# The output gate of the gated linear attention: from the delta-rule stage's woven tiles back into the input projection

## What is computed

```python
for l in range(DEPTH):
    x = layer_norm(ALPHA * x + swiglu_half(x, ffn1...), ln1...)
    h = x @ w_in[l]
    (a_u, a_v, b_qkv, b_z, b_beta, b_decay,
     c_q, c_k, c_v, c_r, c_g) = jnp.split(h, split_at, axis=-1)
    out_a = spatial_gating(gelu(a_u), gelu(a_v), ...)
    out_b = gated_deltanet(b_qkv, b_z, ...)   # ends in: rms_norm(o) * silu(z)
    out_c = gla(c_q, c_k, c_v, c_r, c_g, ...) # ends in: rms_norm(o) * silu(r)
    x = layer_norm(ALPHA * x + concat(out_a, out_b, out_c) @ w_out[l], ln2...)
    x = layer_norm(ALPHA * x + swiglu_half(x, ffn2...), ln3...)
```

## The kernel before

| Stage | Slot | Products before |
|---|---|---|
| form | after the first spreads | 2 |
| form | p = 0, 1, 2, 3 | 3, 3, 3, 5 |
| units | after the mean's sums, after the square's sums | 5, 7 |
| units | after the key transposes (L2206) | 1 |
| units | after the gating's products (L2225) | 2 |
| units | after the scores (L2233) | 4 |
| units | after the outputs (L2240, L2245) | 4 |
| solve | after the first 32x32 products | 1 |
| solve | r = 0, 1, 2, 3 | 2 each |

## Time and profile before

### The profile page before, as it was taken

The page is one execution under the profiler, slowest core; times in us unless marked ns, Lnnn a source line. Parts: engine busy times, 40 slices in busy tenths (PEclk is TensorE's granted clock), DMA queues, the critical chain, the costliest instruction groups (busy, mean ns, idle before and its releaser), DMA issues.

```text
span 3838.6 us, 45043 instructions
## 1 busy us (share of the span) xinstructions
PE 3726.0 (97%) x18720; PEld 3064.0 (80%) x18720; DVE 2073.4 (54%) x3686; ACT 1354.8 (35%) x2088; POOL 86.1 (2%) x164
## 2 busy tenths in 40 slices
PE   8997999999999999999999999999999999999998
PEld 5985669999997678888887767788788877677886
DVE  5936767644457553334336775533553367765335
ACT  4424443222237442322223833322232228333222
POOL 0100001111100000000000000000000000000000
PEclk9998999999999999999999998999999999999999
DMA  6410003433311022233232211222222222112222
GB/s 223 151 61 1 23 23 124 124 129 127 117 64 48 23 88 96 96 108 101 96 99 83 88 45 44 83 99 99 88 96 94 98 88 83 51 50 88 97 96 83
DMA packets 92887, 333.38 MB, mean 87 GB/s; under 512 B 11364, under 2 KB 11532, under 8 KB 92428
## 3 DMA queue, kind: packets, MB, share of 16 engines
q1 hardware_dynamic: 77040, 278.10, 21.7%
q0 software_dynamic: 12800, 41.95, 3.6%
q10 hardware_dynamic: 2844, 10.44, 0.8%
HBM read 328.35 MB, written 2.10 MB: 86 GB/s over the span
## 4 chain that ended last, share of the span: by engine, by line
PE 90%; DVE 6%; ACT 2%; issue 1%; DMA 0%; PEldq 0%; ACTq 0%; DVEq 0%; PEld 0%; SPq 0%
PE PS L552 74%; PE PS L1108 2%; PE PS L554 2%; PE PS L1126 1%; PE PS L1654 1%; PE PS L2134 1%; PE PS L1466 1%; PE PS L1093 1%; PE PS L1009 1%; DVE silu_ctx L2587 1%; DVE arena L2585 1%; DVE H_r L734 0%; DVE XH L906 0%; PE PS L1096 0%; PE PS L1094 0%
## 5 line engine op out<-in xcount | busy, mean ns | idle before, releaser
L552 PE MATMUL PS<-arena_r,ring_hi 128*128 128x512 f32 (+1 forms) x6028 | 2024.1, 375 | 22.8 <-DVE H_r L734 20.2
L552 PE MATMUL PS<-arena_r,ring_r 128*128 128x512 f32 (+1 forms) x4556 | 1701.4, 373 | 0.0
L552 PEld LDWEIGHTS PS<-arena_r,ring_hi 128*128 128x128 f32 x6028 | 1125.9, 188 | 199.3 <-issue 27.3
L552 PE MATMUL PS<-H_r,ring_hi 128*128 128x512 f32 (+1 forms) x3084 | 1151.2, 373 | 0.0
L552 PEld LDWEIGHTS PS<-arena_r,ring_r 128*128 128x128 f32 x4556 | 855.6, 188 | 125.5
L398 DVE TENSOR_TENSOR ring_r<-ring,ring_hi 128x1024 fp32r<-128x1024 f32 x502 | 612.6, 1222 | 603.8 <-ACT ring_hi L389 603.5
L389 ACT ACTIVATE ring_hi<-ring 128x1024 fp32r<-128x1024 f32 x502 | 528.9, 1055 | 864.2 <-DMA ring<-weights_dram 856.2
L552 PEld LDWEIGHTS PS<-H_r,ring_hi 128*128 128x128 f32 x3084 | 580.3, 188 | 89.0 <-issue 2.6
L1823 ACT ACTIVATE arena<-PS 128x512 f32<-128x512 f32 x88 | 52.6, 598 | 519.2 <-PE PS L552 519.2
L1272 DVE SCALAR_TENSOR_TENSOR XH<-PS,mods,XH 128x256 f32<-128x256 f32 (+1 forms) x168 | 79.4, 518 | 232.6 <-PE PS L552 218.3
L353 DVE CAST arena_r<-arena 128x512 fp32r<-128x512 f32 (+1 forms) x184 | 74.2, 403 | 196.8 <-ACT arena L1319 193.7
(11 more groups left out here) (382 smaller groups left out, 3296.6 us busy)
## 6 DMA issues: line engine op xcount, KB each, us to landing
ring<-weights_dram SPq DMA_DIRECT2D x526, 512.0 KB, 3.3
rstd<-ada_later_dram POOLq DMA_DIRECT2D x54, 256.0 KB, 3.0
mean<-ada_later_dram POOLq DMA_DIRECT2D x53, 256.0 KB, 3.0
ada_extra<-ada_later_dram POOLq DMA_DIRECT2D x53, 256.0 KB, 3.0
XH<-xT_dram ACTq DMA_DIRECT2D x1, 3072.0 KB, 20.0
ring<-weights_dram ACTq DMA_DIRECT2D x4, 512.0 KB, 4.0
out_dram<-XH SPq DMA_DIRECT2D x8, 256.0 KB, 2.0
con<-second_dram ACTq DMA_DIRECT2D x1, 1536.0 KB
```

The lines of the kernel that those rows point to most:

```text
L552: ins = pe.matmul(PS[:, o.bank, 0:hi - lo], w[:, 0, :], x, **flags)
```

## The change

The two tiles of `c_r` leave the woven tiles and become two ordinary tiles of `in_plan` (split products, evacuated by ACT with SiLU straight from PSUM), placed ahead of the four GELU tiles. The order of the weights in `stream()` follows, and so do the side jobs of the projection: those that hung on tiles 14 to 18 now hang on tiles 16 to 20, behind the same neighbours as before. Four woven tiles are left, 32 products per layer, on banks 4, 4, 6, 7. The slots are now 2 and 3, 3, 2, 2 in form; 5, 7, 0, 1, 1, 1 in units; 1 and 1, 1, 1, 1 in solve. Two of ACT's six woven copies go (the first operation of `units_act` and the one ahead of the r loop in `solve_act`); the copy of woven tile 1 is therefore made after L2273. `rec_act` has four SiLUs left, none of them at n = 2.

```diff
-WOVEN_COLS = [(2048, 2560), (3088, 3344)]
-WOVEN_BANKS = (4, 4, 6, 7, 6, 7)
+WOVEN_COLS = [(2048, 2560)]
+WOVEN_BANKS = (4, 4, 6, 7)
...
-                s += ftiles(w, (0, 512)) + ttiles(w, (2832, 3088))
+                s += ftiles(w, (3088, 3344)) + ftiles(w, (0, 512)) + ttiles(w, (2832, 3088))
...
-            t[15]["beside_pe"] = gates_pe
+            t[17]["beside_pe"] = gates_pe
...
             t += [ftile(x_x, LAT, "dve", copy_dve(to_lat(d))) for d in (qg, kg)]
+            t += [ftile(x_x, LAT, "act", func_act(to_lat(rg[:, m, :]), ACT.Silu)) for m in range(2)]
             t += [ftile(x_x, LAT, "act", func_act(to_lat(d), ACT.Gelu_apprx_tanh)) for d in (up_[:, 0, :], up_[:, 1, :], vp_[:, 0, :], vp_[:, 1, :])]
...
-        woven_dst = [zp[:, m, :] for m in range(4)] + [rg[:, m, :] for m in range(2)]
+        woven_dst = [zp[:, m, :] for m in range(4)]
...
             ins.then_inc(ga_kt.sem, 1)
-            woven_pe(pe, 1)
             woven_copied_pe(pe, l, 2)
...
             ins.then_inc(sg_z.sem, 1)
-            woven_pe(pe, 2)
+            woven_pe(pe, 1)
...
                 ins.then_inc(ga_s.sem, 1)
-            woven_pe(pe, 4)
+            woven_pe(pe, 1)
...
             ins.then_inc(ga_o.sem, 1)
-            woven_pe(pe, 4)
+            woven_pe(pe, 1)
 
         def units_act(act, l):
 
-            woven_act(act)
             act.wait_ge(sg_mean.sem, sg_mean.next("act"))
...
-                woven_pe(pe, 5 if p == 3 else 3)
+                woven_pe(pe, 3 if p < 2 else 2)
...
                 ins.then_inc(so_z.sem, 1)
-                woven_pe(pe, 2)
+                woven_pe(pe, 1)
...
-            woven_act(act)
             for r in range(4):
                 act.wait_ge(so_z.sem, so_z.next("act"))
```

More of the change, by code:

```diff
@@ L1943, in in_plan @@
             t[13]["beside_act"] = lambda act: l2_roots_act(act)
[L1944 to L1950, removed]
+            t[16]["beside_dve"] = lambda dve: (l2_scale_dve(dve, 1), zero_rows_dve(dve, l))
+            t[16]["beside_pe"] = lambda pe: turn_rows_pe(pe, l)
+            t[17]["beside_act"] = lambda act: (turned_rows_act(act), high_rows_act(act))
+            t[17]["beside_pe"] = lambda pe: turn_keys_pe(pe, l)
+            t[18]["beside_dve"] = lambda dve: (key_rows_dve(dve, l), low_rows_dve(dve))
+            t[19]["beside_pe"] = lambda pe: turn_values_pe(pe, l)
+            t[20]["beside_dve"] = value_rows_dve
             return together(t, 4)
```

## The result

The changed kernel takes 3870.41 us (median of 4 runs, 3869.47 to 3870.91), the kernel before 3841.09 us beside it (4 runs, 3833.71 to 3848.68). The ratio is 1.0076, interval 1.0061 to 1.0091: slower, as forecast, but the forecast of 3861 us is 9.4 us too low and the time lies 0.4 us above the end of the range.

The account below looks back on a forecast made before the run. PE was taken as the bound, busy 97% of the span. From 3840.3 us: projection +21.8, form -5.6, loops -7.4 and +5.2, low clock ahead of the loops +6.6, giving 3861 us; range 3838 to 3870.

Parts of the forecast that it names:

- the loops: Solve loop, both layers: at 0.50 throughout, 23.05 us each against 30.47 and 17.90, so -7.4 and +5.2 us.
- the recurrence behind them: Recurrence after the solve loop: ACT loses two SiLUs at n = 2, where PE doesn't wait for it; nothing.
- low clock from units on without a break: Likeliest case: PE at 0.50 in both layers from units on, through the whole loop; 3861 us, chance 0.45.
- The projection: Projection, on PE's path: two tiles more in each of two layers at 5.44 us a tile, +21.8 us.
- Form: Form's tail: three of five products removed all come off PE's path, 2.80 us per layer, -5.6 us.
- Units: Units: eight products go, 7.5 us of PE, but the chain is DVE's; no saving, PE's waits grow instead.
- The wait ahead of L2240: Units, sign of being right: PE's wait grows from 1.55 to 4.3 us, shown by 3.5 us or more.
- the new wait of 1.72 us for the woven copy: Units, ahead of the state updates: PE newly waits for ACT's copy of woven tile 1, 0.62 us; hidden.
- Ahead of the loops: Between units and solve loop at 0.50: late copies, 32x32 products and scores together +3.3 us per layer, 6.6 us.
- The last rival: Something late in the projection, or recurrence and mix longer at half speed behind the loop: 3868 us or more, chance 0.10.
- chance alone: Rival: clock behaves as in the profile, one loop at each level, the level partly chance; 3845.3 us, chance 0.18.
- The rival that ends below before: Rival: both solve loops run at 1.00, 14.08 us each; 3836.3 us, not slower, chance 0.10.

Follow-up runs that it names:

- e4: Changed kernel without the two gate tiles in the projection, the mix using two of the delta rule's gate tiles instead; 3848.3 us.
- e1: Changed kernel with eight unread full-width filler products (identity as stationary matrix) per layer, in units only, where woven products were taken away; 3867.1 us.
- e2: e1 plus one filler product in each of the solve loop's four rounds, 12 fillers a layer; 3853.25 us.
- e11: e1 with a 128x128 block of X instead of the identity as the fillers' stationary matrix; 3866.5 us.
- e7: Kernel before with one woven product of each solve-loop round moved into units, leaving one a round; median 3839.98 us, ten runs in three groups.
- e5: Changed kernel with one filler product more in each of the solve loop's four rounds, 8 in all, none in units; 3857.67 us.
- e9: Kernel before with form's slot p = 3 cut from 5 to 2 products, the three put into units; 3829.12 us.
- e10: Kernel before with two woven products per layer moved from behind the square's sums to the 32x32 products ahead of the loop, form unchanged; 3831.67 us.
- e8: Kernel before with one filler product more in each solve-loop round, three products a round; 3840.89 us.
- e6: Kernel before, form's p = 3 slot cut from 5 to 2 woven products, one more behind the scores and two at the 32x32 products; 3830.15 us.

## Why the prediction was right in sign and too low

Two terms of the prediction failed: the loops, priced at 23.05 us each, took 26.11 and 25.41, and the recurrence behind them, put at nothing, cost 2.0. Its low clock from units on without a break failed too, at little cost. Term by term:

**The projection: right.** The two rows answer to the earlier trace rows, again 45 starts in 10.20 us, and PE waits for nobody in this stretch:

```profile
2205.64 0.39 PE L552 MATMUL PS<-arena_r,ring_r 128*128 128x512 f32 x1
...
2215.84 0.39 PE L552 MATMUL PS<-arena_r,ring_r 128*128 128x512 f32 x1
```

10.88 and 10.80 us in the two layers; e4 says 22.1 for both, the sum 21.8.

**Form: right, 0.2 us a layer short.** Forecast -2.80, measured 25.95 - 23.36 = 2.59. Timelines of PE and then DVE in the changed kernel, against the earlier trace rows:

```profile
2254.55 2.27 PE L2402 MATMUL PS<-arena 64*128 64x128 f32 x32 [0.73 <-DVE XH L2564]
2256.75 1.98 PE L2135 MATMUL PS<-XH,ring 128*128 128x512 f32 x4
2258.81 1.12 PE L2191 MATMUL PS<-arena,con 128*128 128x512 f32 x2
...
2256.95 1.28 DVE L2570 TENSOR_TENSOR XH<-XH,PS 128x512 f32<-128x512 f32 x2
...
2258.79 0.69 DVE L2294 TENSOR_TENSOR con<-con 128x512 f32<-128x512 f32 x1 [0.56 <-PEq L335]
```

DVE ends at 2256.95 + 1.28 = 2258.23 and still waits 0.56 us, not 0.3. PE ends its two products at 2256.75 + 1.98 = 2258.73. The mis-sized term is the price of a product: 4.66 us over the five of the earlier trace rows also spreads what a run costs once. Two longer runs in units of the same trace give the price of one more:

```profile
2260.63 4.45 PE L2135 MATMUL PS<-XH,ring 128*128 128x512 f32 x10
...
2267.55 6.17 PE L2135 MATMUL PS<-XH,ring 128*128 128x512 f32 x14
```

(6.17 - 4.45) / 4 = 0.43 us an instruction, 0.86 a product and not 0.93; three are 2.58 us, against 2.59 measured. The product removed at p = 2 is hidden, as said: it would have shown as a saving above 2.58.

**Units: no saving, as forecast, but they weren't hidden in layer 0, and the sign named for them failed.** The wait ahead of L2240, forecast at 3.5 us or more, isn't there in layer 0 and is 1.56 us in layer 1; there the one ahead of L2443 is 3.20 us, near the 3.4 forecast. Timeline of PE in the changed kernel, layer 0, then two rows of DVE and one piece of the chain that ended last:

```profile
2276.75 0.79 PE L2215 MATMUL PS<-arena 64*32 64x64 f32 x56 [1.72 <-ACT arena L2149]
...
2284.99 2.08 PE L2135 MATMUL PS<-XH,ring 128*128 128x512 f32 x2
2286.99 5.13 PE L2233 MATMUL PS<-arena 32*128 32x128 f32 x32
2292.06 2.08 PE L2135 MATMUL PS<-XH,ring 128*128 128x512 f32 x2
2294.06 4.54 PE L2240 MATMUL PS<-arena 128*64 128x128 f32 x32
...
2299.50 1.13 PE L2135 MATMUL PS<-XH,ring 128*128 128x512 f32 x2
...
2302.09 0.21 PE L2443 MATMUL PS<-arena,XH 32*32 32x32 f32 x1 [1.47 <-ACT XH L2280]
...
2289.10 0.69 DVE L2337 TENSOR_TENSOR arena<-PS,con 128x512 f32<-128x512 f32 x1 [0.25 <-PE PS L2233]
2290.12 0.69 DVE L2337 TENSOR_TENSOR arena<-PS,con 128x512 f32<-128x512 f32 x1 [0.33 <-PE PS L2233]
...
2276.21 0.50 ACT arena L2149
```

The forecast's sums had the clock fall at that wait. It fell earlier, at 2277.90: the first row is the new wait of 1.72 us for the woven copy, the one that the prediction named and called hidden, and behind it the scores take 5.13 us and fill the time in which a wait had been expected. With the clock low, DVE waits for the scores four times, 1.24 us together (forecast 0.3), which the prediction had named as a sign of being wrong. From the units' start to DVE's last transpose of the inverse it is 39.85 us where before had 38.23. And the chain that ended last no longer is DVE's in layer 0: from the copies at 2274.64, the woven one with 0.50 us among them, it runs through PE's work and ACT's copies of the output to the 32x32 products. In layer 1, where the wait is 1.72 us too, the chain is still DVE's. The new wait also stands just ahead of the fall, where the slot of a product had been. That the wait is the cause isn't shown: e1 puts a product back there, which leaves 0.86 us of the wait, and the stage is still at 0.85; e2 and e11 put one back, the wait is again 0.86 us, and it is at 1.00.

**Ahead of the loops: right in sum, 5.8 us for 6.6,** though by other stages than named: layer 0 lost 2.98 us up to the loop, 2.96 of them before the 32x32 products, layer 1 lost 2.86, 2.90 of them in these. ACT's copies of the output do come late in layer 0, and PE's last row above waits for them:

```profile
2299.64 2.40 ACT L2280 ACTIVATE XH<-PS 64x512 f32<-64x512 f32 x4 [20.57 <-PE PS L2245]
```

They end at 2302.04, and PE goes on at 2302.09. The forecast had both layers low from units on without a break. It wasn't: by the first table the clock was back at 0.99 for layer 0's 32x32 products and at 1.00 for layer 1's outputs, and it fell anew ahead of or in each loop.

**The loops: mechanism right, size too small by 5.4 us.** Both are at 0.50, as forecast; together they take 26.11 + 25.41 = 51.5 us where I had 2 x 23.05 = 46.1. The mis-sized term is the 23.05: it was before's 30.47 less 7.42 for four products, and the earlier trace rows had the clock low only up to 2322.30, not to 2325.28. The loop's end is the same instruction in both kernels, timeline of PE in before and then the chain of the changed kernel:

```profile
2322.33 2.08 PE L2464 MATMUL PS<-XH,arena 64*64 64x64 f32 x32
```

```profile
2311.30 2.00 PE PS L2135 x2
...
2330.27 3.62 PE PS L2463 x32
```

2.08 us at full clock, 3.62 at half, 1.5 more in each loop. With two products a round the clock had come back ahead of the last corner; with one it didn't. I had written that one product in each is less to bring it back, and then used a length in which it had come back. The rest is the price of a product again: at half clock a slot of two takes 3.71 us in the chain and a slot of one 2.00, so four products fewer take 4 x 1.71 = 6.8 us off and not 7.4. Over two loops that is 4.2 of the 5.4 us, and layer 0's loop is 0.7 longer than layer 1's, most of it PE's waiting (1.42 us in the one, 0.87 in the other).

**The recurrence: forecast at nothing, cost 2.0 us.** The low clock now reaches further into it: 25.77 and 26.79 us for 25.24 and 25.27. The windows of layer 1, before (the changed kernel's is the last of the six above):

```profile
3372.34:3397.61 25.27, 24.70 (x209) 22.94 (x209) 12.37 (x27) 10.07 (x19) 0.00 (x0) 0.86 0.01 2
```

The last rival had this mechanism ("at 0.50 behind the loop") and 3868 us or more. It stood beside the likeliest case as another one, but it follows from it: a loop that ends at 0.50 starts the recurrence at 0.50. Taken together the two would have given 3861 + 5.4 + 2.0 = 3868.4.

**The rest.** The first block took 2.56 us more (its own clock, by the two stretches above; the prediction had nothing for it), form gave 0.4 less than forecast, the stages ahead of the loops cost 0.8 less. 20.6 + 5.4 + 2.0 + 2.6 + 0.4 - 0.8 = 30.2, against 30.0 measured.

**The rivals.** The level is not chance alone: of the 61 runs of before beside the experiments 53 lie between 3837 and 3848, which I read as one loop low, five at 3831 to 3834 and three near 3850, while the changed kernel's four lie within 1.5 us, and every profiled loop with one product a round is low. Some of it is chance all the same, as e7's groups and the difference between e1 and e2 in units show. The rival that ends below before needed a loop at 1.00 and got none. The rule of the Trainium skill behind it (TensorE: Matmul & The Clock Gate, "HAM oscillation — how this bites in real kernels", waits between bursts of matmuls lose the clock, and matmuls that follow one another without such a wait keep it) doesn't describe this loop: PE was busy 24.54 of 25.41 us and stayed at 0.50. What e5 changed was the kind of work, eight full-width products more, and its loops were at 0.84 and 0.89.

**What stays open.** Shown: the two tiles cost 22.1 us; a second product in each round gives 12.7 us back; the same products at other places make before itself 11 to 14 us faster. Not shown: what starts the fall. e9 and e10 move different products and both keep the clock, e1 and e2 have the same units, as e1 and e11 have but for data, and fall in different stages, and e7's loop, with one product a round, seems to have stayed up in four runs of ten where the changed kernel's didn't in any of four. Nor was the new wait tried alone.

## What to carry to other kernels

Filler work on an engine that "has slack" isn't free to move: on PE it can also hold the granted clock, and the stage that pays may be two stages further on. Before taking such work away, find the stretches in which the clock sits near its fall, price the loop behind them at both levels, and carry a low clock through to whatever follows. And where a kernel's runs come in steps of one size (here 10 to 13 us), look for one stage that is at full clock in some and at half in others, and try the same work at other places: here that gave 0.3 to 0.4% for moving two or three of 48 products a layer, e9's 3829.12 us being the best.

## What the hardware showed that was not expected

- More matmuls made the changed kernel faster: eight on the path by 12.7 us (e5), twenty-four by 17 us (e2, eight of them on the path).
- PE at 0.50 with no gap: 20.40 of 20.40 us busy in the changed kernel's units. Its work there was mostly of 32 and 64 rows or columns; two full-width products were among it.
- A loop that is entered low costs 25.4 us with one product a round and 17.9 at full clock with two: at half clock, four products fewer are 7.5 us longer.
- Three products a round didn't make the loop safe: e8's two are both at 0.85, while six of six in e6, e9 and e10 with two stayed at 1.00. What matters lies also ahead of the loop.
- What stationary matrix a filler multiplies by, the identity or a block of the data, made no difference to the total (e1 3867.1, e11 3866.5 us).
